# Two of eight weight sums of a fast body move from adding transfers to VectorE, and V's half chunks are spread between the products

## What is computed

```
def odd_layer(x, pre_g, w_in, sink, w_out, post_g):
    h = rms_norm(x, pre_g)
    qc, kc, vc, gc, qd, kd, vd, gd = _split(h @ w_in, ODD_IN_WIDTHS)
    ...
    oc = dilated_mixture_attention(qc, kc, vc.reshape(...))     # three groups of heads
    od, lse = banded_attention(qd, kd, ...)
    mix = jnp.concatenate([oc.reshape(b, s, -1) * jax.nn.silu(gc), od.reshape(b, s, -1) * jax.nn.silu(gd)], axis=-1)
    return x + rms_norm(mix @ w_out, post_g)
```

## Time and profile before

| | us |
|---|---|
| median of 3 runs | 1228.3 |
| lowest, highest | 1227.59, 1230.19 |
| the profiled execution | 1225.88 |
| its span, first to last instruction | 1224.0 |

### The profile page before, as it was taken

The page is one execution under the profiler, slowest core; times in us unless marked ns, Lnnn a source line. Parts: engine busy times, 40 slices in busy tenths (PEclk is TensorE's granted clock), DMA queues, the critical chain, the costliest instruction groups (busy, mean ns, idle before and its releaser), DMA issues.

```text
span 1224.0 us, 15110 instructions
## 1 busy us (share of the span) xinstructions
PE 1183.8 (97%) x5660; PEld 986.8 (81%) x5660; DVE 784.4 (64%) x937; ACT 621.7 (51%) x854; POOL 120.6 (10%) x165
## 2 busy tenths in 40 slices
PE   7999999999999999999999999898998979999997
PEld 6788888888888888788888888786786868888886
DVE  5375546566666954777555558685886858667654
ACT  5554443545545543665445456464565655445442
POOL 2400001200000000010000001310213113000000
PEclk9999999999999999999999999998998999999999
DMA  9994443444445555654445389799797988434541
GB/s 367 254 310 173 166 177 137 176 168 142 172 166 206 201 193 195 229 209 177 172 152 192 137 243 211 267 248 276 235 230 257 252 221 358 158 138 172 176 168 69
DMA packets 39206, 249.39 MB, mean 204 GB/s; under 512 B 4928, under 2 KB 5056, under 8 KB 11632
## 3 DMA queue, kind: packets, MB, share of 16 engines
q1 hardware_dynamic: 31248, 201.34, 45.4%
q0 software_dynamic: 7040, 45.13, 16.7%
q10 hardware_dynamic: 864, 2.18, 0.5%
HBM read 244.44 MB, written 4.19 MB: 203 GB/s over the span
## 4 chain that ended last, share of the span: by engine, by line
PE 74%; DMA 16%; DVE 4%; ACT 3%; issue 2%; POOL 1%; SPq 0%; ACTq 0%; DVEq 0%
PE acc L517 63%; DMA g_turned<-weights 8%; DMA raw<-weights 6%; DVE w_lo L1483 3%; PE bank_x L667 2%; PE acc L724 2%; DMA probs<-x_nat 2%; ACT w_hi L1013 1%; PE bank_x L651 1%; PE bank_y L621 1%; PE acc L735 1%; PE bank_x L597 1%; PE bank_y L597 1%; ACT w_hi L841 0%; ACT w_hi L1001 0%
## 5 line engine op out<-in xcount | busy, mean ns | idle before, releaser
L517 PE MATMUL acc<-w_hi,act_hi 128*128 128x512 f32 x1176 | 466.2, 396 | 2.5 <-DVE w_lo L1186 2.5
L517 PE MATMUL acc<-w_lo,act_hi 128*128 128x512 f32 x1176 | 458.9, 390 | 0.0
L1186 DVE TENSOR_TENSOR w_lo<-raw,w_hi 128x2048 fp32r<-128x2048 f32 x147 | 337.8, 2298 | 161.5 <-ACT w_hi L841 161.3
L841 ACT ACTIVATE w_hi<-raw 128x2048 fp32r<-128x2048 f32 x147 | 281.7, 1916 | 156.4 <-PE acc L517 130.2
L517 PE MATMUL acc<-w_hi,act_lo 128*128 128x512 f32 x1176 | 315.1, 390 | 0.1
L517 PEld LDWEIGHTS acc<-w_hi,act_hi 128*128 128x128 f32 x1176 | 221.1, 188 | 46.9 <-DVE w_lo L1186 3.7
L517 PEld LDWEIGHTS acc<-w_hi,act_lo 128*128 128x128 f32 x1176 | 220.6, 188 | 47.2 <-DVE act_lo L1195 0.5
L517 PEld LDWEIGHTS acc<-w_lo,act_hi 128*128 128x128 f32 x1176 | 221.2, 188 | 42.9
L1483 DVE TENSOR_TENSOR w_lo<-raw,w_hi 128x1024 fp32r<-128x1024 f32 x104 | 125.6, 1246 | 14.8 <-ACT w_hi L1013 14.1
L1013 ACT ACTIVATE w_hi<-raw 128x1024 fp32r<-128x1024 f32 x104 | 104.5, 1051 | 24.8 <-DMA raw<-weights 22.2
L863 ACT ACTIVATE probs<-scores,negm 128x256 f32<-128x256 f32 (+1 forms) x80 | 36.5, 458 | 98.6 <-DVE negm L1273 73.3
(11 more groups left out here) (223 smaller groups left out, 1113.6 us busy)
## 6 DMA issues: line engine op xcount, KB each, us to landing
raw<-weights SPq DMA_DIRECT2D x175, 1024.0 KB, 4.8
raw<-weights POOLq DMA_DIRECT2D x32, 1024.0 KB, 12.0
g_turned<-weights SPq DMA_DIRECT2D x24, 512.0 KB, 9.9
resid<-x_turned SPq DMA_DIRECT2D x8, 256.0 KB, 9.3
mix<-rpb POOLq DMA_DIRECT2D x32, 64.0 KB, 23.8
postg<-post_g POOLq DMA_DIRECT2D x2, 1024.0 KB, 26.7
resid<-x_perm POOLq DMA_DIRECT2D x2, 1024.0 KB, 8.2
x_kept<-resid POOLq DMA_DIRECT2D x2, 1024.0 KB, 4.3
```

Source lines behind the costliest of these rows:

```text
L517: m = nc.tensor.matmul(tiles[t][:, :], a[:, kt, t * P:(t + 1) * P], w[:, buf, kk * NB:(kk + 1) * NB], start=(kt == 0 and a is act_hi and w ...
L841: nc.scalar.activation(w_hi[:, at % SPLIT, :], raw[:, at % RAW, :], ACT.Copy).then_inc(S["hi_ready"], 1)
L1186: nc.vector.tensor_tensor(w_lo[:, at % SPLIT, :], raw[:, at % RAW, :], w_hi[:, at % SPLIT, :].bitcast(F32), ALU.subtract).then_inc(S["lo_r ...
```

## The change

- The order is now a list FAST_SEQ of 22 slots with V's half chunks as entries of their own, and the halves stand between other products: W11 W11 V0a V0b W21 V1a V1b P P V2a W22 V2b W22 Q Q W21 R R V3a T T V3b. The last number of an entry is its block. V1, V2, W21's second chunk and V3 use block 4.
- Splits go by pieces (half chunks; the first four as two whole chunks) in a ring of six. The piece p goes into slot h if piece p - 6 was used in slot h - 1. W11 of the next body is so split in slots 20 and 21.
- Q's two sums are made by VectorE: in slots 6 and 7, behind their pieces, it adds block 3 to block 0 and block 2 to block 1 (P + W22), on the chip. Six adding transfers a body are left. The adds for R wait for this as well.
- From the second fast body on GpSimd starts P's two adds between the two rotations.
- ScalarE copies the turned q and k of these units, and not VectorE.
- Loads by SyncE follow the new order. One semaphore for halves is gone; buffers and blocks behind the fast bodies are counted by chunk_buf and chunk_raw.

```diff
+FAST_SEQ = (("W11", 0, None, 0), ("W11", 1, None, 1), ("V", 0, 0, 2), ("V", 0, 1, 2), ("W21", 0, None, 3),
...
+FULL = 4
+AHEAD = 2 * SPLIT
+FAST_N = len(PIECES) - FULL // 2
+BY_DMA, BY_DVE = ("P", "R", "T"), ("Q",)
+def counted(piece):
+    return piece // 2 + 1 if piece < FULL else piece + 1 - FULL // 2
...
+def at_slot(h):
+    if h == 0:
+        return [FULL, FULL + 1]
+    return [p for p in range(AHEAD, len(PIECES) + FULL) if PIECES[p - AHEAD][0] == h - 1]
...
# SyncE
-                load(2, d + 6, op + 3)
-                load(3, d + 7, op + 4)
-                load(4, d + 10, op + 7)
-                load(4, d + 3, op + 12)
-                load(2, d + 11, op + 13)
+                load(2, d + 7, used("V", 0))
+                load(3, d + 6, used("W21", 0))
+                load(4, d + 10, used("V", 1))
+                load(4, d + 3, used("V", 2))
+                load(4, d + 11, used("W21", 1))
                 d += BODY
                 if k < FAST - 1:
-                    load(3, d + 9, op + 14)
-                    load(4, d + 2, op + 15)
-                    load(0, d, op + 16)
-                    load(1, d + 1, op + 17)
-                    load(2, d + 8, op + 18)
+                    load(3, d + 2, used("R", 0))
+                    load(2, d + 8, used("R", 1))
+                    load(0, d, used("T", 0))
+                    load(1, d + 1, used("T", 1))
+                    load(4, d + 9, used("V", 3))
...
# GpSimd
+                    def first_sums():
+                        add_weights(0, 4, counted(last_piece("W11", 0)))
+                        add_weights(1, 5, counted(last_piece("W11", 1)))
                     for k, (blk, cols) in enumerate(turns):
+                        if u.kind == "G" and u.body > FAST0 and k == 1:
+                            first_sums()
                         pool.wait_ge(S["proj_ready"], PROJ0[layer] + 3 * u.body - 2 + k)
...
+                        if u.body == FAST0:
+                            first_sums()
+                        for c in range(2):
+                            pool.wait_ge(S["q_added"], 2 * (u.body - FAST0) + c + 1)
+                            add_weights(3 - c, 4 + c, counted(last_piece("W22", c)))
+                        for c in range(2):
+                            add_weights(c, 2 + c, counted(last_piece("Q", c)))
...
# ScalarE
+                for p in at_slot(h):
+                    act.wait_ge(S["chunk_used"], op + (counted(p - AHEAD) if p >= AHEAD else 0))
+                    half_buf = (2 * RING * RAW + p) % AHEAD
+                    if p >= len(PIECES):
+                        if p % 2:
+                            r = (p - len(PIECES)) // 2
+                            act.wait_ge(landed[r], 16 * (RING + FAST_COUNT[r] * (k + 1) + 1))
+                            nc.scalar.activation(w_hi[:, half_buf // 2, :], raw[:, r, :], ACT.Copy).then_inc(
+                                S["hi_ready"], 1)
+                        continue
...
# VectorE
-                    if h == 20:
-                        dve.wait_ge(S["chunk_used"], op + 17)
+                    if h == 21:
+                        wait_for("T")
                         dve.wait_ge(S["c11_taken"], k + 1)
...
                     attention(u, h)
                     fast_split(u, h)
+                    if h in (6, 7):
+                        c = h - 6
+                        add_from = 3 - c
+                        dve.wait_ge(S["lo_ready"], op + counted(last_piece("P", c)))
+                        dve.wait_ge(landed[add_from], fast_landings(k, FAST_SEQ.index(("W22", c, None, add_from))))
+                        nc.vector.tensor_tensor(raw[:, c, :], raw[:, c, :], raw[:, add_from, :], ALU.add).then_inc(
+                            S["q_added"], 1)
```

More of the change, by code:

```diff
@@ L1016, in fast_body @@
+                    cols = slice(half_buf % 2 * 2 * NB, (half_buf % 2 + 1) * 2 * NB)
+                    nc.scalar.activation(w_hi[:, half_buf // 2, cols], raw_part(r, half), ACT.Copy).then_inc(S["hi_ready"], 1)
             def fast_body(u):
                 k, op = u.body - FAST0, first_op(1, u.body)
-                for h in range(len(FAST_SLOTS)):
+                for h in range(FAST_SLOTS):
                     if h == 0:
```

215 lines of the change are left out of this document (105 added, 110 removed), and 3 rows, old and new, of the table FAST_SEQ.

## The result

| | before | after |
|---|---|---|
| median of 4 runs | 1227.9 us | 1251.9 us (1249.9 to 1253.9) |
| ratio | | 1.0193, 95% interval 1.0170 to 1.0215 |
| profiled execution (span) | 1225.9 (1224.0) | 1253.9 (1252.0) |
| four fast bodies | 297.9 us | 323.5 us |

What follows compares the result with a forecast made beforehand. TensorE, busy 97% of the span, was taken as the bound. Four bodies at full rate, 264.8, plus 12, 33 and 3 gave 312.8 us against 297.9: +14.9, a median of 1243, range 1212 to 1262.

Steps and rivals of the forecast that it cites:

- A body at full rate: One fast body without stalls or slow clock: 66.2 us, four 264.8, against 297.9 for the four before the change.
- VectorE's sums at 0: Q's additions on VectorE, slots 6 and 7, 2.3 us each, were expected to cost no time; at most 2.3 a body.
- TensorE, no longer the DMA engines, would be the bound.: Per fast body, two adds less cut transfers from 68.1 to 57.9 us, below TensorE's 66.2.
- The landings: Mid-body times worked out for issuing R's and T's additions and for W21's second chunk and V3 to land.
- The middle: Mid-body, late W21 second chunk and V3 plus slower clock: 3 us a body, 12 in all; bounds 0 and 6.
- The boundary: Between fast bodies, late second low part, rotation, clock and late first chunk: 11.0 us at each of three; bounds 4.5 and 14.
- The late first chunk: At a boundary, the next body's first chunk loads only after T's first chunk is split: 2.7 us taken.
- The boundary to the next kind of body: After the last fast body, the low part comes later than wanted, without P adds: 3.0 us; bounds 1 and 6.
- Equal turns: Rival: plain blocks get half the engines beside adds, so W21 and V3 are in time; -6.7, 1222 us; chance 0.17.
- The cheap boundary: Rival: rotation 2.3 us, nothing late, clock holds, 4.5 a boundary, no middle loss; -18.6, 1210 us; chance 0.13.
- the whole gain: Rival: something releases W11 and the rotation in time at the boundary; 1197 us; chance 0.05.
- The rule on SBUF: Two-input VectorE and SBUF-reading GpSimd instructions exclude each other; rotation steps would wait, 2.8 us more a boundary, 8.4 in all.

Runs made afterwards that it cites:

- e4: Changed kernel with Q's two weight sums made again by additions of the DMA queue, not by VectorE: 1250.3 us.
- e3: Changed kernel with GpSimd's order at the boundary put back, both rotations and then P's two additions: 1253.3 us.
- e1: Changed kernel with R's sum in a PSUM bank of its own, so no take is waited for (computes another result): 1245.6 us.
- e5: Changed kernel with VectorE's takes of the sums of P, Q and R one slot earlier in its list: 1251.5 us.
- e2: Changed kernel with the next body's second W11 chunk split before, not after, the close of the attention unit in slot 21: 1244.7 us.
- e9: Changed kernel with R's first addition, and the three behind it, issued only when W21's second chunk has landed: 1255.1 us.
- e6: Changed kernel with T's two additions issued only when W21's second chunk has landed: 1262.2 us.

## Why the prediction was right in sign and 9 us short

- **A body at full rate, 66.2 us; VectorE's sums at 0.** The first body of after ran its first 15 slots without a wait in 45.4 us (721.08 to 766.5), where the working had 45.3; a whole body without a wait no run shows. The zero for the sums stood: an addition took 2.28 us (forecast 2.3), and undoing them changed nothing.
- **"TensorE, no longer the DMA engines, would be the bound."** Wrong, and this is the step behind the rest. I added up 57.9 us of transfers against 66.2 of TensorE over a whole body. Without the two additions the engines idle in the stretch that these had filled, and from 751 to 778 they are full either way (1.02 without them, 1.00 with them in e4); a mean over the body could not show it.
- **The landings.** The times worked out from the rows were good. Counted from the body's start, R's and T's four additions were issued at 28.3, 33.4, 35.5 and 39.4 (forecast 27.8, 32.8, 35.2, 39.0), W21's second chunk was split at 45.5 (44.6) and V's fourth at 57.7 (55 to 56).
- **The middle, 3 us a body.** This is the term that failed. The first body, with no boundary ahead of it, took 77.06 where 66.2 is full rate: 10.9. The other three, from V's first product on, took 71.1, 70.0 and 69.5 against 60.0 (66.2 less 6.2 for what stands ahead of V): 11.1, 10.0 and 9.5, of which 1.6, 0.8 and 0 are slower clock at V's start. So the middle cost 9.2 to 10.9 a body, 39 in all, above my upper bound of 6 a body. I had asked only whether TensorE would find V's fourth chunk split. I did not ask what stands behind it in VectorE's list: T's low parts and the take of R, which TensorE needs before T because Q, R and T share a bank. Of the first body's 10.9 us, 6.5 are TensorE's waits at W21's second chunk, R and T (1.0, 2.1, 3.4), and the clock adds to it: after the 3.36 us without work, 786.2 to 791.8 had a granted clock of 0.50 (1.2 GHz), which costs 2.8 us in that stretch, as these windows of after show beside one that follows a wait of 2.13 us:

```profile
773.40:778.00 4.60, 4.57 (x24) 3.95 (x25) 2.90 (x3) 0.03 (x1) 0.00 (x0) 1.00 0.97 360
786.20:791.80 5.60, 5.52 (x14) 4.26 (x15) 2.83 (x3) 0.00 (x0) 4.17 (x4) 0.50 0.95 372
```

- **The boundary, 11.0.** The order of events stood line by line, but the term was too large. V began 11.7, 12.5 and 11.7 after the start (forecast 12.8), 5.5, 6.3 and 5.5 more than the 6.2 of full rate (forecast 6.6), and slower clock cost 1.6 (809.8 to 815.8 at 0.74), 0.8 and 0 us (forecast 1.7). The late first chunk, 2.7 us of the 11.0, cost nothing there: its low part was done 1.2 to 1.4 us before each body began, since the middle had already made TensorE late. 6.5 on average instead of 11.0, 20 in place of 33.
- **The boundary to the next kind of body, 3.0.** TensorE waited 1.8 us there, behind the end of the four bodies.
- **Together.** Forecast 12 + 33 + 3 = 48 over full rate; measured 39 + 20 + 2 = 61. The boundaries gave back 13 and the middle took 27 more, so it is in part luck that the sum is as near as it is: two terms are off in opposite directions, one of them by more than a factor of three. In the profiled executions the kernels differ by 28.0, in the medians by 23.9, and the forecast of the median is 9 short.
- **The rivals.** Equal turns is excluded: with additions queued W21's second chunk took 16.6 us from its issue (750.03) to its first high part. The cheap boundary is excluded as a forecast of the time, 1210, but its price of 4.5 a boundary is nearer to the measured 6.5 than my 11.0. For the whole gain I wrote 1197, where my own terms give 1228.3 - 33.1 = 1195. The rule on SBUF holds at the boundary, but in e3 it is the close, not the rotation, that pays.
- **What I named as signs.** Three bodies were forecast at 78 to 82 us and took 82.7, 82.5 and 81.2, two of them above. The sign for too small a middle, over 3 us at V's fourth chunk, stood one slot further on, at T, with 2.7 to 3.4 us.

Why e1 gained 6 us and e5 nothing, with the same two waits removed, the first body shows in part. In e1 V's fourth chunk was split 57.7 us after the body's start and the next first chunk was asked for at 63.3, as in after (57.7 and 63.4); in e5 it was 59.2 and 65.7. What stays open is what the copies on ScalarE cost, what T's sum on VectorE gives without the wait for the plain load, and how the 39 us of the middle divide over all four bodies between the takes, the landings and the clock.

## What to carry to other kernels

A sum moved off a transfer queue is worth what its stretch is worth: over the four bodies, one addition a body out of the stretch where the queue is full gave 12.6 us, and two a body out of a stretch that became idle gave nothing, in two kernels. Compare demand and supply between the time at which a buffer comes free and the time at which its next block is needed, not over a loop body. And when a wait is forecast on an engine that works in order, walk down its list: the next instructions, here the take that frees a bank, are late as well. Removing the wait that the profile names can merely lay bare the next one, and an instruction moved forward in the list delays what it passes (in e5 20.9 us of waits gone, no time gained).

## What the runs showed of the hardware

- A GpSimd rotation beside VectorE's close made the close 6.0 us long in e3 and 7.0 in e2, in place of 4.6; one instruction on 8 words a partition took 0.73 us in place of 0.17. In e5 three of T's low parts beside the rotation took 4.30 us together, 1.43 each, where two in after took 2.35. In after V's first four low parts took 6.72 us beside the rotation (from 804.18), in e3 4.62 without it (from 802.10).
- Making the additions wait for one plain load of 1 MB, which then landed within 4.8 us (e9: asked for at 749.26, the first addition issued at 754.05), did not bring the next plain block forward (779.54 against 778.79). Leaving the engines at a share of 0.31 from 765 to 770, in the full stretch, went with 10 us more over four bodies (e6).
- In after, with additions queued, the same plain load took 16.6 us from its issue to its first high part, and the four additions issued from 749.41 on took 10.8, 11.8, 14.7 and 16.4 us to land, against 7.9 for the one issued at 716.15.
